# Two-layer token-mixer and expert kernel: the preparation ahead of the experts in another order

## What is computed

```python
for i in range(2):
    sh1, sc1, g1, sh2, sc2, g2 = split(silu(c) @ mod_w[i] + mod_b[i])   # modulation
    h = modulate(rms_norm(x), sh1, sc1)
    y = concat(conv(h), retention(h), attention(h)) @ w_out[i]          # output projection
    x = x + g1 * y
    h = modulate(rms_norm(x), sh2, sc2)
    scores = sigmoid(h @ router_w[i])
    idx = top_k(scores + router_b[i], 6)                                # 6 of 64 experts
    w = 2.5 * scores[idx] / sum(scores[idx])
    x = x + g2 * (sum_k w_k * expert_idx_k(h) + shared_expert(h))       # swiglu experts
```

## Time and profile before

| what | us |
|---|---|
| median of 3 executions | 2405.94 (2404.68 to 2408.18) |
| the profiled execution's own time | 2402.2 |
| its span in the profile | 2400.4 |
| PE busy | 2174.2 (91%) |
| DVE busy | 910.6 (38%) |
| ACT busy | 566.3 (24%) |
| POOL busy | 674.1 (28%) |
| layer 0: output projection starts, experts start | 460.62, 672.85 |
| layer 1: output projection starts, experts start | 1651.52, 1786.86 |

### The profile page before, as it was taken

The page is one execution under the profiler, slowest core; times in us unless marked ns, Lnnn a source line. Parts: engine busy times, 40 slices in busy tenths (PEclk is TensorE's granted clock), DMA queues, the critical chain, the costliest instruction groups (busy, mean ns, idle before and its releaser), DMA issues.

```text
span 2400.4 us, 36613 instructions
## 1 busy us (share of the span) xinstructions
PE 2174.2 (91%) x12802; PEld 1173.2 (49%) x12802; DVE 910.6 (38%) x1858; ACT 566.3 (24%) x1170; POOL 674.1 (28%) x811
## 2 busy tenths in 40 slices
PE   4998989898899999999997798899879998888997
PEld 1464344454555555555546463354355454444545
DVE  2186676315512222222226485663352211111117
ACT  4222154304211111111113522342211111111113
POOL 0000000000245555555540000000045555555530
PEclk8999999998899999999999899999989999999999
DMA  7522000018699999999969121000159999999977
GB/s 317 221 78 75 0 1 1 1 35 333 240 376 418 420 412 408 408 409 418 412 266 326 53 91 37 1 1 18 70 236 397 417 416 414 409 408 409 413 295 245
DMA packets 104857, 594.23 MB, mean 248 GB/s; under 512 B 25142, under 2 KB 29374, under 8 KB 62528
## 3 DMA queue, kind: packets, MB, share of 16 engines
q1 hardware_dynamic: 68656, 524.73, 54.1%
q0 software_dynamic: 34672, 63.07, 7.0%
q10 hardware_dynamic: 1440, 5.24, 0.6%
HBM read 572.94 MB, written 60.56 MB: 264 GB/s over the span
## 4 chain that ended last, share of the span: by engine, by line
PE 68%; DMA 18%; DVE 7%; ACT 3%; issue 2%; SPq 1%; POOL 0%; POOLq 0%; DVEq 0%; ACTq 0%
PE psum L1056 22%; PE psum L704 18%; DMA arena<-in_experts 13%; PE psum L1078 10%; PE psum L875 3%; PE psum L899 2%; DMA arena<-y 2%; PE psum L915 2%; DMA arena<-in_mod_w 2%; PE psum L787 2%; PE psum L813 2%; PE psum L1064 1%; DVE arena L1544 1%; PE psum L720 1%; PE psum L1122 1%
## 5 line engine op out<-in xcount | busy, mean ns | idle before, releaser
L1056 PE MATMUL psum<-arena 128*64 128x256 f32 x6144 | 715.5, 386 | 39.2 <-DMA arena<-in_experts 31.2
L1056 PEld LDWEIGHTS psum<-arena 128*64 128x64 f32 x6144 | 440.4, 138 | 252.6 <-issue 43.6
L704 PE MATMUL psum<-arena 128*128 128x512 f32 (+1 forms) x1360 | 503.7, 528 | 24.9 <-ACT arena L1180 12.7
L2085 POOL DMA_INDIRECT arena<-hrows,IX x384 | 394.1, 1026 | 228.1 <-POOL IX L2081 163.1
L704 PEld LDWEIGHTS psum<-arena 128*128 128x128 f32 x1360 | 259.6, 193 | 264.1 <-issue 235.0
L1078 PE MATMUL psum<-arena 128*64 128x512 f32 x1536 | 363.5, 593 | 6.9 <-DMA arena<-in_experts 5.7
L2093 POOL DMA_INDIRECT y<-arena,IX x192 | 197.1, 1027 | 305.7 <-DVE arena L1929 146.2
L1936 DVE TENSOR_TENSOR arena<-psum,arena 128x128 f32<-128x128 f32 x192 | 55.9, 291 | 503.9 <-ACT arena L1420 503.9
L1420 ACT ACTIVATE arena<-psum 128x128 f32<-128x128 f32 x192 | 53.3, 278 | 667.6 <-PE psum L1056 667.6
L1428 ACT ACTIVATE arena<-psum 128x512 f32<-128x512 f32 x192 | 114.7, 597 | 310.7 <-PE psum L1078 310.7
L1078 PEld LDWEIGHTS psum<-arena 128*64 128x64 f32 x1536 | 112.8, 137 | 144.1 <-issue 119.8
(11 more groups left out here) (245 smaller groups left out, 1740.2 us busy)
## 6 DMA issues: line engine op xcount, KB each, us to landing
arena<-in_experts SPq DMA_DIRECT2D x128, 2048.0 KB, 20.9
arena<-in_experts SPq DMA_DIRECT2D x128, 1024.0 KB, 23.7
arena<-in_mod_w SPq DMA_DIRECT2D x48, 1024.0 KB, 11.1
arena<-y SPq DMA_DIRECT2D x20, 1536.0 KB, 15.6
arena<-in_wblk SPq DMA_DIRECT2D x22, 1024.0 KB, 4.9
arena<-in_shared SPq DMA_DIRECT2D x2, 3072.0 KB, 10.4
arena<-hrows,IX POOLq DMA_INDIRECT x384, 8.0
hrows<-arena ACTq DMA_DIRECT2D x10, 512.0 KB, 8.7
```

Of the source, the lines that this page charges most:

```text
L704: last = mm(job(l, key, n, parts), a, b, start=i == 0, stop=i == len(pairs) - 1)
L1056: last = mm(psum[j * ROWS:(j + 1) * ROWS, (0, 1, 5)[u], 0:2 * P], HT[:, u, k, :], w[:, k * 512 + j * 256:k * 512 + (j + 1) * 256], start=k ...
L2085: g.indirect_dma_start(GR[:, r, h * 256:(h + 1) * 256], None, rows, offsets(IX[:, s, h:h + 1]), bounds_check=4 * T * P - 1, oob_is_err=Fal ...
```

## The change

Four edits, and the new order that they need:

- Layer 1's modulation products, with their DMAs, move from the shared-expert stage into layer 0's output projection, one behind each job and eight behind the last; their six weight slots move to the part of `arena` that attention used, so their loads start when attention is over.
- The mask is made by replacing the six largest scores with a constant (`match_replace`; two of the eight found values are first lifted to one that occurs nowhere, constant `drop`) and comparing with the scores. The one-hots follow later. `"rank"` moves ahead of the shared expert's products; those stand between `"rank"` and the tables, and behind the tables.
- The squares of the second norm are summed inside the output projection; `product` can wait for H chunk by chunk (`arrived`), for the first input products, and the router's products wait so too.
- ACT loads the tables of Sqrt and Sigmoid with a one-column operation ahead of their use; the picks of destinations are made for half the tiles at once, the weights of the six experts behind the tables; POOL reads its first five table columns ahead and issues two index copies before the first gather.

The core of the diff:

```diff
+        for m in range(KC):
+            for s in sq:
+                self.after.append(("wo", m, s))
                 while waiting:
-                    self.shared.append(waiting.pop(0))
-                g = beside.pop(0)
-                self.shared.append(g)
-                if g[3] == KC - 1:
-                    self.shared.append(("md",) + g[1:3])
-                    waiting.append(("mt",) + g[1:3])
+                    self.after.append(waiting.pop(0))
+                tiles(1)
+            if m:
+                self.after.append(("squares", m - 1))
+        tiles(2)
+        self.after.append(("squares", KC - 1))
+        self.after += [("n2", s) for s in sq]
+        while waiting:
+            self.after.append(waiting.pop(0))
+        tiles(3)
+        self.after += [("bc", "n2", s) for s in sq]
+        tiles(len(beside))
+        self.after += [("rl", s) for s in sq] + ["router"]
+        j += [(x, "D" if x[0] in ("wo", "bc") else "A") for x in self.after if x[0] not in ("mod", "squares")]
...
+        self.shared = ([("md", 1, 2)] if l == 0 else []) + sum(hr[:4], []) + ["rank"]
         if l == 0:
-            self.shared.append(("su", 1, 0))
-        tiles(1)
-        for t in range(t_out):
-            self.shared += [("hr", t, i) for i in range(2)]
-            tiles(1)
-            if l == 0 and t >= 3:
-                self.shared.append(("oh", t - 3))
-        self.shared += [("oh", t) for t in range(3 if l == 0 else 0, t_out - 1)] + ["tab"]
-        tiles(1)
-        self.shared.append("ix")
-        if l:
-            self.shared.append(("su", 1, 0))
-        for s in sq[1:]:
-            for k in range(2):
-                self.shared.append(("sg", k, s))
-                tiles(1)
-                self.shared.append(("su", k, s))
-                tiles(1)
-        tiles(len(beside))
-        self.shared += waiting
+            self.shared += sum(hr[4:], []) + [("mt", 1, 2), "signs", ("sg", 0, 1), "eid", ("sg", 1, 1), ("su", 0, 1), ("su", 1, 1)]
+            self.shared += oh + ["tab", "ix", ("sg", 0, 0), ("su", 0, 0), ("sg", 1, 0), ("su", 1, 0)]
+        else:
+            self.shared += ["signs", ("sg", 0, 0), "eid", ("sg", 1, 0)] + oh + ["tab", "ix", ("su", 0, 0), ("su", 1, 0)]
...
+                outs = [g for g in weights if g[:2] == (l, "out")]
+                load_weights(outs[0:2])
...
-                load_beside(range(21))
+                sp.wait_ge(sem("at_cat"), groups_before(l) + len(attn_groups(l)))
+                load_beside(range(8))
+                load_weights(outs[2:3])
+                load_beside(range(8, 12))
+                load_weights(outs[3:4])
+                load_beside(range(12, 16))
+                sp.dma_start(WB[2], A["shared"][l]).then_inc(sem("shared_in"), 16)
+                load_beside(range(16, 24))
...
+                    if b == 1:
+                        sp.wait_ge(sem("hrow"), 16 * (pl.t_out + 6 * l))
                     if b == 2:
-                        ready(sp, l, ("su", 1, pl.sq[-1]))
+                        ready(sp, l, ("su", 1, 0))
...
+                        if arrived is not None:
+                            pe.wait_ge(sem(f"h_ready{l}"), arrived + i + 1)
...
+                    first = {("g", 0, 0): 0, ("g", 0, 1): KC, ("rk", 1): KC}.get(key)
+                    product(key, P, [(blk[:, k, :], H[:, k, a:a + n]) for k in range(KC)], n, first)
...
+                            for k in range(KC if s == st[1] else 0):
+                                pe.wait_ge(sem(f"h_ready{l}"), KC * (2 + i) + k + 1)
...
+                table(ACT.Sqrt, 1)
+                for st in pl.after:
+                    if st[0] == "wo":
...
+                        evacuated(act, l, st)
+                        act.wait_ge(sem(f"sq_used{l}"), at - 2)
+                        f(SQB[:, at % 3, 0:n], X[:, k, a:a + n], ACT.Square).then_inc(sem(f"sq_ready{l}"), 1)
+                    elif st[0] == "n2":
+                        root(st, SEG[st[1]][1] // 4)
+                    elif st[0] in ("md", "mt"):
+                        ready(act, l, st)
+                        mod_rows(st) if st[0] == "md" else mod_columns(st)
+                table(ACT.Sigmoid, 2)
...
+                link(V.tensor_tensor(rt[:, 0:T, 3, :], rt[:, 0:T, 0, :], c("drop").unsqueeze(1).to_broadcast([P, T, 8]), ALU.max))
+                for t in range(T):
+                    last = V.match_replace(GEB[:, t, :], rt[:, t, 3, :], sel[:, t, :], -3e38)
+                link(last)
+                V.tensor_tensor(MSK[:, 0:T, :], GEB[:, 0:T, :], sel, ALU.not_equal).then_inc(sem("mask"), 1)
...
-                    V.reduce_sum(MSK[:, ts, :], one_hot(ts).rearrange("p (t k) e -> p t e k", k=TOPK), AX
-                                 ).then_inc(sem("mask"), 1)
-                pick(2, SC, halves[0])
-                shared_hidden(0, 0)
...
+                if l:
+                    one_hots()
...
+                V.tensor_tensor(DST[:, 0:T, :], rank, every(1), ALU.add).then_inc(evacD, 1)
+                evacuated(dve, l, "rank")
+                link(V.tensor_tensor(DST[:, 0:T, :], DST[:, 0:T, :], GEB[:, 0:T, :], ALU.add))
...
+                if l == 0:
+                    one_hots()
+                for ts in halves:
+                    pick(3, DST, ts)
+                for t in range(T):
+                    last = V.tensor_copy(dsti[:, t, 0:TOPK], rt[:, t, 3, 0:TOPK])
+                link(last)
...
-                    if t == 2 and l == 0:
-                        shared_hidden(1, 0)
-                    pick(3, DST, slice(t, t + 1))
-                    link(V.tensor_copy(dsti[:, t, 0:TOPK], rt[:, t, 3, 0:TOPK]))
-                    V.tensor_scalar(LOHI[:, 0, :], dsti[:, t, 0:TOPK], P - 1, None, ALU.bitwise_and)
-                    link(V.tensor_scalar(LOHI[:, 1, :], dsti[:, t, 0:TOPK], 7, None, ALU.arith_shift_right))
...
+                    if t == 1 and l == 0:
+                        for j in range(2):
+                            shared_hidden(j, 1)
...
+                first = [table_column(s, 0) for s in range(5)]
+                pool.wait_ge(sem("hrow"), 16 * (T + 6 * l))
+                pool.wait_ge(sem("tab_ready"), l + 1)
+                for x in ((0, 1), (2, 3, 4)):
+                    for s in x:
+                        indices(s, 0, first[s])
+                    for s in x:
+                        gather(s, 0)
```

217 lines of the change are left out of this document (108 added, 109 removed).

## The result

The changed kernel takes 2375.6 us (median of 4 runs, 2369.7 to 2380.0) against 2405.3 us (4 runs, 2401.4 to 2408.2) for the one before: ratio 0.9871, 95% interval 0.9852 to 0.9891, 30 us less. The profiled execution has a span of 2374.0 us against 2400.4, so 26.4 us are to be found in the traces. The forecast of 2380 us was 4 us too high, well inside its range of 2366 to 2395. The sum inside it was 26 us; the 4 us are the 3.7 us between profiled execution and median, which are not there this time (2376.0 us against 2375.6).

What follows compares the result with a forecast made beforehand. PE was taken as the limit in layer 0's experts, the DMA weight stream in layer 1's. Gains 9 + 1 + 16 = 26 us off 2402.2 give 2376.2, plus 3.7 to the median: 2380 us, range 2366 to 2395.

Steps and rivals of the forecast that it cites:

- First products: Input projections, both layers: waiting chunk by chunk starts PE earlier, 4.5 us each, 9 us together (8.8 to 15).
- Layer 0, output projection to experts: Waits of 19.6 us against 20.2 before; gain 0 to 3 us, taken as 1 (bounds -5 to +5).
- Layer 0's combine stage: Transposing and adding expert results in layer 0: the prediction had no term for it, 0 us.
- Layer 1 to the router: Output projection to router: one table load less, router matmuls following the shifts chunk by chunk; 3 us.
- Router to the issue: Layer 1, router's end to issue of weight slots 2 and 3: 47.8 us instead of 58.8, 11 us earlier.
- Issue to end: Layer 1 after the issue of slots 2 and 3: weight stream without the hole of 1805 to 1815 us; 2 us.
- Rival 1, the clock,: New shared stage runs at the 1.2 GHz level: 7 us lost over both layers, 2387 us; chance 0.18.
- Rivals 2 and 3: PE carries layer 1, array warm everywhere: 2361 us, chance 0.08; layer 1's gain is hidden: 2394 us, chance 0.11.
- Rival 4: Tables come no earlier, say with MATCH_REPLACE at its upper bound, leaving products behind them bare: 2429 us; chance 0.06.
- Signs: Traces: layer 1 tables end 29 to 33 us after router, issue at 48, 410 GB/s; layer 0 experts within 5 us.

Runs made afterwards that it cites:

- a_rank: Changed kernel with layer 0's rank products in PSUM bank 7 instead of bank 3: 2369.9 us, ratio 0.9846.
- a_mix: Changed kernel with shared products between the table products, two in layer 0 and one in layer 1: 2374.9 us, ratio 0.987.
- b_bank: Kernel before, PSUM bank count moved on by five from layer 0's shared down projections, giving combine jobs the changed kernel's banks: 2403.5 us, ratio 0.9977.
- a_bank: Changed kernel, bank count moved on by two from layer 0's shared down projections, giving combine jobs their old banks: 2383.2 us, ratio 0.9892.
- a_order1: Changed kernel with two of layer 1's four shared products ahead of transposes and rank products again, as before: 2384.5 us, ratio 0.9906.
- a_mask: Changed kernel with the mask made by sums over one-hot rows again, in both layers: 2387.7 us, ratio 0.9917.
- a_recip: Changed kernel with DVE making the roots of both segments in layer 0 before scaling the first: 2364.8 us, ratio 0.9819.
- a_best3: Changed kernel with a_recip's and a_rank's edits, a layer 0 gate product between table products, one more modulation product beside the output projection: 2358.5 us, ratio 0.9804.

## Why the prediction was right, and where it wasn't

- **First products: 9 us forecast, 12 found.** The start moved by 4.4 us in layer 0 and 3.9 in layer 1, near the 4.4 worked out. Undersized was the upper part of the term, "if the shorter pause leaves the array fast": in layer 1 it mostly does (7.10 us against 10.08), in layer 0 it doesn't (8.80 against 9.46).
- **Layer 0, output projection to experts: +1 forecast, -6.6 in the profile**, -2 to -3 in the two traces without its slow stretch. Every wait came near its forecast, 21.1 us against 19.6. The step that failed is the work between them: "PE does the same work before and after the change", with "2.4 us more" for the three modulation products behind the 8.1 us pause. By the records, waits left out, three things are missing from it. First, the sixteen products of the output projection take 85.5 to 85.6 us with a modulation product behind each, in all ten traces of the new order, and 82.8 before; the prediction has this 0.4 us a pair in its check of the loads and not in its sum. Second, the shared product behind the 4.8 us pause lost 2.3 us (5.94 against 3.62 in a_rank), and of the four behind the tables the first takes 9.2 us and the others 6.9 to 7.0. Third, the six table products take 14.2 us, where they took 12.3 before (and take 8.9 in a_mix). Unpriced on the other side: the sums, the spreads and the router's products take 3.6 us less than before.
- **Layer 0's combine stage: nothing forecast, 7.6 found.** The prediction followed which instructions move and not which banks they land on. It used that for one job (the bank of `"rank"`, 4.1 us forecast, 4.8 found) and not for the jobs behind. b_bank and a_bank show the cause from both sides.
- **Layer 1 to the router: 3 forecast, 1.1 found.** The waits for the spread (2.5), the shifts (1.2), the squares (1.1) and the copy (0.8) are still there, and the output projection's products, which now have the sums between them, take 56.3 us instead of 55.1.
- **Router to the issue: 11 forecast, 9.5 found**, 6.7 of it by the order (a_order1), and a mask by sums would cost 5.2 of it (a_mask); the two overlap. The 1.5 us missing are slow products and a wait: 0.7 us up to the end of the tables (8.83 us for 7.1, and 2.2 us of wait ahead of `"eid"` where 0.7 were forecast) and 0.8 behind them (14.89 us for 14.1).
- **Issue to end: 2 forecast, 3.6 found.** No hole is left in the stream (422 and 415 GB/s where the earlier trace rows had 319). But that the issue of slots 2 and 3 sets the end is only half true, as a_mix shows: there it is 4.6 us earlier, and the end stays. The refill of slot 0 comes 16 us behind the issue and, by the rows of a_mix, hangs on the tables, by way of the gathers. In the changed kernel that refill comes early enough for the stream to go on, so the forecast wasn't hurt.
- **Rival 1, the clock,** had the right mechanism. Against the shortest rows of the same products in the other traces, layer 0's new shared stage loses some 10 us and layer 1's some 4. Not all of this is beyond the forecast, since the tables were slow before too, but it is as large as the 7 us that the rival asked for; unforeseen gains elsewhere hid it. The Trainium skill, "TensorE: Matmul & The Clock Gate", section "HAM oscillation", was drawn on for it in the form that waits between bursts bring the clock down. For the 8.15 and 4.81 us pauses the trace agrees: the clock granted behind them is 0.79 (581 to 593 us) and 0.69 (609 to 616 us). For the table stage it doesn't say what is seen: the four slow products have one wait of 0.42 us, and PE is busy for 10.55 of the 11 us from 630 to 641.
- **Rivals 2 and 3** are refused: layer 1 still waits 34.6 us for weights (26.8 and 7.8 us; before, 31.2 and 5.4, of which the prediction names the first), and its end did come earlier, by 13.1 us counted from the router. **Rival 4** is refused by the tables at 32.2 us and by MATCH_REPLACE at 0.21 us.
- **Signs.** The tables' end, the issue, the 415 to 422 GB/s, the two named waits and the modulation loads came as said. "Within 5 us" for layer 0's experts was missed in the profiled execution (6.6 us) and holds in a_bank and a_order1.
- **Not tested by themselves** are the squares summed inside the output projection, the tables of Sqrt and Sigmoid loaded ahead, the picks by halves and POOL's early index copies. Their part in the gain is open.

## What to carry to other kernels

Where buffers are dealt out by a running counter, a change of the order anywhere is a change of every later job's buffer: list each job's bank and who held it last, before and after, ahead of any other reading. The Trainium skill, "Perfetto Trace Analysis", section "Matmuls", says that independent groups of matmuls should rotate through the banks; one pair of neighbours on the same bank made PE wait 7.35 us here, in a kernel that rotates nearly everywhere else. When small operations are laid between large ones, price what the large ones lose: 2.8 us over sixteen products here. When a chain on another engine bounds a stage, look at what it makes for others and how late: one root, made behind 16 scalings that nobody waited for yet, kept PE idle for 8 us, and ahead of them it took 7.5 us out of the stage (a_recip). And a shortcut in one resource (weights issued 4.6 us earlier in a_mix) was worth nothing here while the second one due at the same time (tables, gathers) did not move as well.

## What the runs showed of the hardware

- **A stage of small products ran at the low clock though PE was all but always busy.** The table stage of layer 0 in the changed kernel, by the view by stretches:

```profile
630.00:641.00 11.00, 10.55 (x49) 10.32 (x48) 6.43 (x10) 0.00 (x0) 0.00 (x0) 0.52 0.80 340
```

  PE is busy for 10.55 of 11 us with 68-column products and is granted 0.52, its 1.2 GHz level. Ahead of this stretch stand two table tiles at 1.45 and 1.55 us with waits of 1.20 and 0.42 us behind them. What brought the clock down, those waits or the small products, no run separates, but 10.5 us of these products did not bring it back. With shared products of 512 columns between them the stage is granted 0.93 in layer 0 and 1.00 in layer 1 (a_mix). In a_mix's layer 0 the shared product behind the second tile is itself slow (8.78 us for 7.1), and the two tiles behind it take 2.79 us together: there the wide product ran through the slow stretch and the tiles did not.
- **The same wait leaves the array fast in one execution and slow in the next.** After 2.2 us of pause ahead of `"eid"` the next product takes 8.83 us in the changed kernel and 7.13 in a_mix. From the first product to layer 0's output projection, the same instructions take 404 to 407 us in eight traces (the changed kernel and a_best3 among them) and 409.5 to 409.8 in five (b_bank, a_rank and a_mask among them). Between the changed kernel and a_rank the difference comes in three places, each behind a wait: 1.3 us at 134 us, 2 from 231 to 238 and 1 at 440. A gain of under 5 us is therefore read from one stretch between two landmarks, and from more than one trace.
